# Both scatter halves in one piece, an undivided gather and fewer mixing slots in a two-layer mixture-of-experts trunk

## The reference

```python
for l in range(DEPTH):                      # DEPTH = 2, D_MODEL = 1024
    h = rms_norm(x, norm_mix_g[l])
    proj = h @ w_in[l]                      # 1024 x 7492
    # three token mixers (gMLP, sparse attention, short conv) -> ya, yb, yc
    merged = g0 * (ya @ w_proj_a) + g1 * (yb @ w_proj_b) + g2 * (yc @ w_proj_c)
    x = x + merged @ w_out[l]
    h = rms_norm(x, norm_ffn_g[l])
    # top-1 of 4 groups, then top-2 of 8 experts inside it; 32 experts
    for each expert e with its tokens xb:
        hid = silu(xb @ w_gate[e]) * (xb @ w_up[e])     # 1024 -> 512
        out[tokens] += weight * (hid @ w_down[e])       # 512 -> 1024
    x = x + out
```

## Time and profile before

| | us |
|---|---|
| median of three runs | 1387.93 |
| lowest and highest | 1385.76, 1388.62 |
| the profiled execution, as timed | 1388.38 |
| its span, first to last instruction | 1385.9 |
| TensorE busy in it | 1367.3 |
| the 16 DMA engines' main queue, share of the span | 87.9% |

### The profile page before, as it was taken

One profiled execution on the slowest core, in us unless ns is written; L12 is line 12 of the kernel. 1 busy time (PEld: TensorE's weight loads), 2 busy tenths in 40 slices (PEclk: granted clock), 3 DMA queues, 4 the chain that ended last, 5 costly groups with the idle time before them and its releaser, 6 DMA issues. The chain is left out here.

```text
span 1385.9 us, 18830 instructions
## 1 busy us (share of the span) xinstructions
PE 1367.3 (99%) x7801; PEld 803.3 (58%) x7801; DVE 584.4 (42%) x945; ACT 386.0 (28%) x707; POOL 16.6 (1%) x44
## 2 busy tenths in 40 slices
PE   9999999999999999999999999999999999999997
PEld 8899888544444444444488988884444444444442
DVE  7796646632222222222278956466222222222223
ACT  6555443211111111111164553441111111111112
POOL 0000000100000000000000000010000000000000
PEclk9999999999999999999999999999999999999999
DMA  9645668999999999999975557599999999999996
GB/s 307 225 166 184 245 227 313 413 405 427 426 427 428 428 426 427 429 426 420 406 239 187 213 186 269 184 381 397 420 424 429 428 427 427 428 426 429 424 421 256
DMA packets 89676, 490.26 MB, mean 354 GB/s; under 512 B 10686, under 2 KB 13816, under 8 KB 58872
## 3 DMA queue, kind: packets, MB, share of 16 engines
q1 hardware_dynamic: 89488, 489.03, 87.9%
q10 hardware_dynamic: 104, 0.03, 0.0%
HBM read 487.99 MB, written 1.05 MB: 353 GB/s over the span
## 5 line engine op out<-in xcount | busy, mean ns | idle before, releaser
L2172 PE MATMUL psB<-slots,uT 128*64 128x512 f32 x2016 | 455.7, 595 | 0.3 <-DVE uT L1588 0.2
L2172 PEld LDWEIGHTS psB<-slots,uT 128*64 128x64 f32 x2016 | 140.3, 137 | 263.8 <-issue 259.9
L2182 PE MATMUL psC<-slots,ybT_plain 128*64 128x512 f32 x1024 | 233.0, 598 | 1.6 <-DMA slots<-in_expert_w_down_dram 0.9
L1249 DVE TENSOR_TENSOR parts<-slots,parts 128x2048 fp32r<-128x2048 f32 (+1 forms) x80 | 177.7, 2249 | 70.1 <-ACT parts L1006 69.2
L1006 ACT ACTIVATE parts<-slots 128x2048 fp32r<-128x2048 f32 (+1 forms) x80 | 148.3, 1888 | 98.0 <-PE psB L1817 52.5
L1645 DVE TENSOR_TENSOR x<-x,psA 128x1024 f32<-128x1024 f32 x60 | 73.3, 1222 | 211.9 <-PE psA L2222 211.9
L1113 ACT ACTIVATE rel_parts<-psC 128x512 fp32r<-128x512 f32 x62 | 37.1, 598 | 385.5 <-PE psC L2182 210.5
L1817 PE MATMUL psB<-parts,hT_parts 128*128 128x512 f32 x448 | 139.0, 391 | 0.9 <-DVE tmp L1526 0.5
L2182 PEld LDWEIGHTS psC<-slots,ybT_plain 128*64 128x64 f32 x1024 | 68.8, 136 | 117.5 <-issue 111.3
L1588 DVE TENSOR_TENSOR uT<-psA,g_ffn 128x512 f32<-128x512 f32 x64 | 44.3, 692 | 163.1 <-PE psA L2133 162.8
L1817 PE MATMUL psA<-parts,hT_parts 128*128 128x512 f32 x320 | 99.5, 392 | 0.0
(11 more groups left out here) (373 smaller groups left out, 1379.1 us busy)
## 6 DMA issues: line engine op xcount, KB each, us to landing
slots<-in_expert_w_down_dram SPq DMA_DIRECT2D x44, 2048.0 KB, 22.5
slots<-in_expert_w_gate_dram SPq DMA_DIRECT2D x40, 2048.0 KB, 22.9
slots<-in_expert_w_up_dram SPq DMA_DIRECT2D x40, 2048.0 KB, 21.7
slots<-in_w_in_dram SPq DMA_DIRECT2D x56, 1024.0 KB, 5.2
slots<-in_expert_w_gate_dram SPq DMA_DIRECT2D x44, 1024.0 KB, 10.5
slots<-in_expert_w_up_dram SPq DMA_DIRECT2D x42, 1024.0 KB, 10.5
slots<-in_expert_w_down_dram SPq DMA_DIRECT2D x28, 1024.0 KB, 10.7
slots<-in_expert_w_down_dram SPq DMA_DIRECT2D x24, 512.0 KB, 10.4
```

Of the source, the lines that this page charges most:

```text
L1249: v.tensor_tensor(low_part, mix_slot(i), high_part, ALU.subtract).then_inc(low_dve, 1)
L2172: ins = te.matmul(psB[j * BLK:(j + 1) * BLK, o, :], xT[:, 4 * half + c, j * BLK:(j + 1) * BLK], w, start=half == 0 and c == order[0], stop ...
L2182: ins = te.matmul(psC[j * BLK:(j + 1) * BLK, n, :], hidT[:, 2 * k + c, j * BLK:(j + 1) * BLK], w[:, c, n * 512:(n + 1) * 512], start=k == ...
```

## The change

In the expert stage, (1) PE does gate half 0 and gate half 1 in a row and then scatters both halves in a row; the upper half goes to `psC`, the down products' banks, and its rounded parts have a tile of their own, `y_second`, in the memory of `first_rows`. (2) The upper half's rounding on ACT waits for the end of the down products (`pair_freed`) where it waited for the lower scatter, and DVE makes its low part before it adds the lower half. (3) The gather's half 1 is done in one piece of six terms ahead of down half 0. (4) In the last two pairs the upper scatter no longer stands between the up halves and the transposes; PE waits for DVE's add there instead. In the mixing stage, (5) a raw slot is reused after four uses from use 32 on (`LEAST_FROM`), and a high slot after three (`HIGHS_FROM`). (6) The raw slot and the high slot so freed are filled with expert weights at uses 32 and 33: 1 MiB, and two halves of 1 MiB for slot 2. (7) The first load into `first_rows` in layer 1 also waits for the last scatter that reads it.

```diff
-    FEWER_FROM = 30
+    FEWER_FROM, LEAST_FROM = 30, 32
     def raw_before(i):
-        return i - (RAWS if i < FEWER_FROM else RAWS - 1)
+        return i - (RAWS if i < FEWER_FROM else RAWS - 1 if i < LEAST_FROM else RAWS - 2)
+    HIGHS_FROM = 32
+    def high_before(i):
+        return i - (HIGHS if i < HIGHS_FROM else HIGHS - 1)
     def high_slot(i):
+        while i >= HIGHS_FROM:
+            i = high_before(i)
+        y_second = rounded("first_rows")[:, :].rearrange("p (a n) -> p a n", a=2)
...
                     if s == 0:
+                        if l:
+                            sp.wait_ge(scatter_ps[1], done)
                         load_first(s)
...
+                    if i == LEAST_FROM:
+                        load_raw(LEAST_FROM - RAWS + 1)
+                    if i == HIGHS_FROM + 1:
+                        wait_used(sp, l, HIGHS_FROM - HIGHS)
+                        load_rest(2)
+                        load_early(2)
...
                 load_first(2)
-                load_raw(MIX_SLOTS - 5)
...
                     if i == MIX_SLOTS - 1:
                         load_early(0)
-                        load_early(2)
-                    load_high(i)
+                    if i > MIX_SLOTS - HIGHS:
+                        load_high(i)
                     load_raw(i)
...
                         if i >= HIGHS:
-                            wait_used(act, l, i - HIGHS)
+                            wait_used(act, l, high_before(i))
...
                     if not first:
-                        act.wait_ge(scatter_ps[0], g)
-                        y_rounded(g - 1, 1, y_main)
+                        act.wait_ge(pair_freed, g * STAGES)
+                        y_rounded(g - 1, 1, y_second)
...
                     if not last:
+                        y_rest(g, 1, y_second)
                         add_half(g, 0, psA)
-                        y_rest(g, 1, y_main)
-                        add_half(g, 1, psA)
+                        add_half(g, 1, psC)
...
-                    elif not last:
-                        pe.wait_ge(x_added, g * 2 + 2)
                     pe.wait_ge(y_dve, g * 2 + n + 1)
+                    ps, y = ((psA, y_main), (psB, y_final) if last else (psC, y_second))[n]
...
                     gate_up(i, 0, tail)
                     pe.wait_ge(xT_done, g * 2 + 2)
+                    gate_up(i, 1, tail)
                     if not first:
-                        scatter(g - 1, 0)
-                    gate_up(i, 1, tail)
-                    if gather_next and not first:
-                        scatter(g - 1, 1)
+                        for n in range(2):
+                            scatter(g - 1, n)
...
                     else:
-                        scatter(g - 1, 1)
+                        pe.wait_ge(x_added, g * 2 + 1)
...
                     if gather_next:
-                        gather(1, terms=range(0, 2))
+                        gather(1)
                     pe.wait_ge(hidT_act, g * 2 + 1)
                     down(i, 0, tail)
-                    if gather_next:
-                        gather(1, terms=range(2, len(GATHER_TERMS)))
                     pe.wait_ge(hidT_act, g * 2 + 2)
                     down(i, 1, tail)
```

More of the change, by code:

```diff
@@ L736, in load_high @@
                     wait_used(sp, l, i)
-                    if high_slot(i) in FIRST:
-                        load_rest(high_slot(i))
-                        return
                     load_main(high_slot(i))
@@ L1672, in pair_rest @@
                         gathered_half(g + 1, 0)
-                    else:
-                        add_half(g - 1, 1, psA)
                     if beside_down:
@@ L1735, in vector_program @@
                     pair_rest(start + i, True)
-                add_half(start + LAST - 2, 0, psA)
-                y_rest(start + LAST - 2, 1, y_main)
+                add_rows(start + LAST - 2)
                 choose_next(LAST - 1, start + LAST - 1)
@@ L1746, in vector_program @@
                     gathered(start + i + MAIN_PAIRS - 1)
-                    add_half(start + i + MAIN_PAIRS - 2, 0, psA)
-                    y_rest(start + i + MAIN_PAIRS - 2, 1, y_main)
+                    add_rows(start + i + MAIN_PAIRS - 2)
                     choose_next(i + MAIN_PAIRS - 1, start + i + MAIN_PAIRS - 1)
@@ L2210, in scatter @@
                 def scatter(g, n, last=False):
-                    ps = psB if last and n else psA
-                    y = y_final if last and n else y_main
                     if n == 0:
                         pe.wait_ge(selT_act, g + 1)
-                    elif not last:
-                        pe.wait_ge(x_added, g * 2 + 2)
                     pe.wait_ge(y_dve, g * 2 + n + 1)
+                    ps, y = ((psA, y_main), (psB, y_final) if last else (psC, y_second))[n]
                     for t in range(NT):
```

## The result

The changed kernel takes 1405.12 us (median, 1400.37 to 1406.75); the kernel before 1387.05 beside it. The ratio is 1.0119, with a 95% interval of 1.0103 to 1.0135: slower by 16.5 us, give or take 2.2. The forecast was 1400.2, that is +12.3.

The account below looks back on a forecast made before the run. Transfers were taken to bound the expert stage's end, and PE mixing. Stall 9.6, half clock 3.3 and earlier loads −0.6 sum to +12.3 us on the 1387.93 median: 1400.2 us, range 1390.5 to 1406.

Parts of the forecast that it names:

- the fourth rival: Two half-clock stretches per layer, and delayed gathers in first pairs uncovering transfers: 1404 to 1407 us, chance 0.11.
- What bounds: Expert stage's end is set by transfers, 29.3 us a pair against PE's 27.38; in mixing PE sets the time.
- The pairs' savings: Scatters and gather in one piece save PE 0.45 to 0.65 us a pair; counted as none, hidden by transfers.
- Part 5, the gap: Mixing, ahead of use 36: PE stalls 4.8 us once a layer, 9.6 us in all, for the read of psB.
- The clock: Behind each layer's gap, one 3.40 us stretch at half clock costs 1.67 us; +3.3 us in all.
- Part 6, the transfers: Expert loads 2 MiB sooner gain 0.5 us in layer 0, 0.1 or none in layer 1; −0.6 us taken.
- the balance at down half 0 of the first pair: Queued transfers of 1.5 us, less 1.0 us of later slot freeing by the whole gather, leave 0.5 us gain in layer 0.
- My bound for the delay alone: Upper bound for part 6: only the later gather's delay counts, twice 1.0 us, +2.
- Part 4: Last two pairs: PE waits for DVE's add, at most 1.2 us in each; taken as 0.
- The head start in full: Rival: queue does not run dry in the first pair, layers end 4.9 us sooner each; 1391 us, chance 0.10.
- the PE rival: PE bounds the expert pairs, so savings of 16 us show: some 1385 or 1383 us, chance 0.06.
- no stall: Rival: in mixing the reading of psB is not held up; only −0.6 remains, 1387.3 us, chance 0.05.

Follow-up runs that it names:

- light_undone: Changed kernel without parts 5 and 6, middle pairs' doubled expert loads bringing only half their bytes (results wrong): 1373.13 us, ratio 0.9893.
- no_high_cut: Changed kernel with the four high slots kept to the end, raw slots still cut: 1400.00 us, ratio 1.0083.
- mix_alone: Kernel before with parts 5 and 6 alone, the pairs as before: 1403.03 us, ratio 1.0114.
- order_fixed: Changed kernel, ACT making the merged high part before rounding use 37, DVE reading psB before use 37's low part: 1389.61 us, ratio 1.0016.
- combined: Changed kernel with order_fixed's program order, first pair's gather divided, and part 4 taken back: 1389.04 us, ratio 1.0000.
- mix_undone: Changed kernel with parts 5 and 6 taken back: 1389.09 us, ratio 1.0013.
- undone_tail: Changed kernel without parts 5 and 6, gather divided in each layer's first pair, part 4 also taken back: 1388.25 us, ratio 0.9995.
- spin: Changed kernel with 21 products of no use on PE filling the gap ahead of use 36: 1398.81 us, ratio 1.0084.

## Why the prediction was right, and where it was off

The sum said +12.3 us and the ratio gives +16.5, give or take 2.2, so the sum is too low by more than the noise. The 1405.12 us lie above the 1396 to 1404 that had a chance of 0.68 and inside the fourth rival, "more is lost", 1404 to 1407, with 0.11; the range held because it took this rival in, and its upper end, 1406, is only 0.9 away. The direction and the main cause, one stall of PE a layer with half clock behind it, came as forecast; the size did not.

**What bounds.** Right. The pairs' savings were put at 0.45 to 0.65 us each and at nothing in the sum; they are 0.65, `light_undone` shows them, and under full transfers they turn into waits for DMA for the reason in the earlier trace rows. The parts of this saving were less well split: eight scatter products in a row take from 502.35 to 504.32 in `light_undone`, 1.97 us, so this saves 0.2 and not 0.3, and the rest, 0.45, belongs to the gather and the down halves that now follow each other.

**Part 5, the gap.** 4.8 us a layer was forecast and 4.63 and 4.91 came, by the chain that was worked out, link by link. One step of it was incomplete. I put the late rounding down to the high slot alone, and said that the later loads land ahead of it. They do, by some 1.5 us (215.50 against 216.98), but only because the high slot is later still. `no_high_cut` shows that the raw slot's cut makes 3.2 us of gap by itself.

**The clock.** The mechanism was right, the size was not: I took one stretch of half clock a layer, 1.67 us, 3.3 in all. There were two on end in each layer, and PE was busy for 5.15 and 6.08 us of them, which costs 5.6. Two were my upper bound, and the first half of the fourth rival. This mis-sized term is 2.3 of the 5.4 us by which the spans' 17.7 is above my 12.3; the expert stages are 2.3, 0.65 is the start of this execution, and some 0.1 is left over.

**Part 6, the transfers.** Forecast −0.6, found +1.7 over the two expert stages of this execution. The step that does not hold in layer 0 is the balance at down half 0 of the first pair. I had 1.5 us of queued transfers there against 1.0 us of later freeing, and let the difference stand as a gain. The first half of this came: ahead of the freeing, loads land 2 us sooner, measured from the stage's begin (282.71 for 276.20, with 8.47 us of shift). But then the queue is empty, and it stays so until PE frees the next slots, 0.9 us later than before. The load there lands after 5.0 us, as one with nothing ahead of it (5.1 in the earlier trace rows):

```profile
286.43 0.80 SPq L612 DMA_DIRECT2D slots<-in_expert_w_up_dram  x2
```

```profile
slots<-in_expert_w_up_dram SPq DMA_DIRECT2D x1, 1024.0 KB, 5.0
```

```profile
286.00:288.00 2.00, 2.00 (x12) 0.70 (x10) 1.62 (x6) 0.00 (x0) 0.00 (x0) 1.00 0.45 107
```

For 2 us the engines are at a share of 0.45 (0.90 in the 2 us from 277.50 in the kernel before). The loads that follow land 8.7 us later than before, and the last of the layer, at 696.47 for 687.50, 9.0 later, which is the 0.5 us of the stage. In layer 1 it is 1.2 of the 1.3. Here loads that came sooner only made the queue run dry sooner. My bound for the delay alone was twice 1.0 us, and 1.7 is near it. But this delay is not shown to be the whole cause: within layer 0 of this execution the landings wander from 0.9 us sooner to 0.7 later than before, counted from the stage's begin; `mix_alone` has +0.9 and +0.7 without the undivided gather, and `order_fixed` has only +0.5 and −0.2 with it. That the head start brings nothing is shown by `combined` and by `order_fixed` beside `mix_undone` (1.0016 and 1.0013); where the 1.7 comes from stays open.

**Part 4** was taken at 0 with 1.2 in each pair as the bound. No wait for the add shows; what came is a wait that I had not named, 0.85 to 0.94 us for `hid` (`ybT_plain` in the rows), which DVE writes behind the up halves while PE has nothing to do in between. At full transfers `undone_tail` shows no price for it that the time can tell.

**The head start in full and the PE rival** both fell, each by an experiment of its own (`combined`, `mix_undone`); the "no stall" rival fell with the trace.

## What to carry to other kernels

When a buffer is taken away, look not for who waits for it but for what stands behind the waiting instruction in program order on the same engine, above all a read that frees a PSUM bank: here the order of two instructions on ACT and two on DVE was worth 14 us, and with the new order the two fewer buffers cost nothing measurable. Where a stage is bound by transfers, ask what work taken off PE in it can be worth: here 0.65 us a pair was worth 12 us with light loads and nothing at full load. Of loads issued sooner, ask whether the queue still holds anything at the next point where it waits for a free slot; here it did not, and 2 MiB sooner brought nothing measurable. Where two waits release one instruction, undoing one of them shows only the difference between the two.

## What the runs showed of the hardware

The half clock behind a gap is not a fixed price. A gap of 4.63 us was followed by PE at half clock until 229.2 in `mix_alone`, 3.1 us of its work, and until 232.1 in the changed kernel, 5.15 us of it, with the same program in mixing. The gap of 4.91 us in layer 1 had the longer stretch in both kernels. The shorter gaps of `no_high_cut`, 3.21 and 3.38 us, had the shorter stretch in both layers:

```profile
225.30:228.40 3.10, 2.92 (x7) 2.37 (x8) 3.00 (x4) 0.97 (x1) 0.00 (x0) 0.50 0.92 357
...
914.80:917.90 3.10, 3.10 (x8) 2.42 (x8) 3.03 (x3) 1.62 (x1) 0.00 (x0) 0.50 0.68 267
```

The Trainium skill, TensorE: Matmul & The Clock Gate, HAM oscillation, says that the change of level is paid again at each such wait. The runs agree: each of the gaps of 3.2 us and more ahead of use 36 was followed by half clock, 0.50 in the rows. Filling the gap with useless products gave back 5 to 6 us, although use 36 began as late behind use 35 as with the gap. Near the end of mixing 3.4 us at half clock come and go with no gap of that length ahead of them: in layer 1 of the kernel before, in layer 0 of the changed one and of `spin`, and nowhere in `mix_undone`, `order_fixed` and `combined`.
